# The last of four channel tiles of a causal convolution, moved from TensorE to VectorE

## The chip, the cores and the metric

The kernel runs on one core of a Trainium2 chip. The metric is the device time of one execution in microseconds, the median of several runs. The engines of the core are called PE (TensorE), DVE (VectorE), ACT (ScalarE), POOL (GpSimd) and SP (SyncE, which only issues DMAs here). Each runs its own list of instructions in order, and they meet at semaphores.

## What is computed

The program is a two-layer decoder trunk over 512 positions of 1024 channels, in float32. The first layer mixes with a state-space branch and a convolution branch side by side, the second with attention; after each mixer comes a norm, then a mixture of 64 experts (MoE) and another norm. The change lies in the convolution branch of the first layer, which works on 512 channels:

```
def conv_branch(v, cv_w, cv_b, ln_g, ln_b):
    val, gate = jnp.split(v, 2, axis=-1)
    h = val * jax.nn.sigmoid(gate)
    h = lax.conv_general_dilated(h, cv_w[:, None, :].astype(h.dtype), (1,), [(CONV_WIDTH - 1, 0)],
                                 dimension_numbers=('NWC', 'WIO', 'NWC'),
                                 feature_group_count=D_CONV) + cv_b
    return jax.nn.silu(layer_norm(h, ln_g, ln_b))

def even_mixer(x, w_in, b_in, ...):
    h = x @ w_in + b_in
    y_a = s5_branch(h[..., :D_S5], ...)
    y_b = conv_branch(h[..., D_S5:], cv_w, cv_b, cv_ln_g, cv_ln_b)
    return jnp.concatenate([y_a, y_b], axis=-1) @ w_out
```

The convolution is depthwise, causal, 31 taps wide: each output channel at position s is the sum of 31 products of one weight and the same channel at positions s-30 to s, plus a bias. The MoE after it scores 64 experts for every position and takes the best eight, so how many blocks of rows it works through depends on the data.

## The kernel before

Everything is kept channel by position: a tile is 128 channels (partitions) by 512 positions, so the 512 channels of the convolution are CT = 4 channel tiles, t = 0 to 3. The first mixer has three stages, each a function with a block of its own. A block ends in a barrier of all five engines, so the next one starts when the slowest engine is through.

**even_in_project** makes the input products on PE. For every convolution tile two products (gate, then value) are made; ACT takes the sigmoid of the gate (L1200) and DVE multiplies it with the value (L1312) into e.h2. This is a pair of buffers in which the tile is kept for PE: 64 channels stand twice in the 128 partitions of one buffer, the second copy shifted by one position, so that one matmul contracts over two taps. So DVE writes each tile with four instructions on 64 partitions. After the last product PE makes the last group of small matmuls (L1144), which ACT copies out (L1188).

**s5_and_conv** holds the state-space branch and the convolution. On PE in this order: the products into the states (L1372), conv(0), then within and across (L1391, L1401) for both halves of the states, then conv(1), conv(2), conv(3). conv(t) is 2 x 16 matmuls (L1382) of a 128 by 64 diagonal matrix of taps with the 512 positions, summed in one PSUM bank; the trace has two records for each. DVE builds the diagonals (L1434, two instructions a tile), works through the state chain twice (L1448 to L1463), and then builds the diagonals of tiles 1 to 3. ACT copies each convolution tile out of PSUM with the bias added (L1422, L1425). SP sends the results of the state-space branch to memory and back to change their layout (L1352, L1356).

**even_finish** sums the four convolution tiles on PE for the mean (L1494), and has the gated product (L1505), the variance (L1502), the norm and the activations. Then the MoE part begins.

Of the kernel before, what the change touches and what calls it, by code (L numbers as in the profile page):

```python
# [11 lines left out]
ALU, ACT, AX = mybir.AluOpType, mybir.ActivationFunctionType, mybir.AxisListType  # L12
# [5 lines left out]
P = 128  # L18
SEQ, D, NT = 512, 1024, 4
# [4 lines left out]
HP = P // 2  # L24
# [967 lines left out]


DS5, G, GS, NS = 512, 32, 16, 64
TAPS, CT = 31, 4
NJ = G * NS // P
LC = P // GS
NCH = SEQ // LC
NPAIR = (TAPS + 1) // 2
# [3 lines left out]
TWO_PI = 6.283185  # L1003

COLS = {}
for _name, _n in (("b_in", 12), ("b_glu", 4), ("cv_b", 4), ("ln_g", 4), ("ln_b", 4), ("taps", CT * 2 * NPAIR),
                  ("lam_re", NJ), ("lam_im", NJ), ("log_dt", NJ), ("skip", CT), ("power", LC + 1), ("chunk_time", NCH),
                  ("ident2", HP)):
    COLS[_name] = (sum(b - a for a, b in COLS.values()), sum(b - a for a, b in COLS.values()) + _n)
# [3 lines left out]
def even_layout(w):  # L1013

    col = lambda v: np.ascontiguousarray(v.reshape(-1, P).T)
    state = lambda v: v.reshape(NJ, P).T
    across = lambda v: np.repeat(np.asarray(v, np.float32)[None, :], P, 0)
    taps = np.concatenate([w["cv_w"][0], np.zeros((1, DS5), np.float32)]).reshape(NPAIR, 2, CT, 2, HP)
    parts = [col(w["ev_b_in"][0]), col(w["s5_b_glu"][0]), col(w["cv_b"][0]), col(w["cv_ln_g"][0]), col(w["cv_ln_b"][0]),
             taps.transpose(1, 4, 2, 3, 0).reshape(P, CT * 2 * NPAIR),  # L1020
             state(w["s5_lam_re"][0]), state(w["s5_lam_im"][0]),
             state(np.repeat(w["s5_log_dt"][0][:, None], NS, 1)), col(w["s5_d"][0]),
             across(np.arange(LC + 1)), across(LC * np.arange(NCH)), np.tile(np.eye(HP, dtype=np.float32), (2, 1))]
    b = np.stack([w["s5_b_re"][0], w["s5_b_im"][0]])
    c = np.stack([w["s5_c_re"][0], w["s5_c_im"][0]])
    b = b.reshape(2, NJ, P, GS).transpose(2, 0, 1, 3)
    c = c.transpose(0, 1, 3, 2).reshape(2, NJ, P, GS).transpose(2, 0, 1, 3)
    return np.ascontiguousarray(np.concatenate(parts, axis=1)), np.ascontiguousarray(b), np.ascontiguousarray(c)
# [24 lines left out]
def even_in_project(nc, g, w, e):  # L1053
    with Part(nc, "evin") as s:
# [3 lines left out]
        sig = s.sb("sig", [P, 2, SEQ])  # L1058
        names = ("dt", "ld", "th", "km", "k", "r", "rho", "are", "aim", "den", "rden", "fre", "fim", "t1", "t2", "t3", "t4")
        v = {n: s.sb(n, [P, NJ]) for n in names}  # L1060
# [4 lines left out]
        bank = [s.ps(f"bank{k}", [P, 512]) for k in range(8)]  # L1065
# [4 lines left out]
        sig_ready, h_ready = s.sem("sig_ready"), s.sem("h_ready")  # L1070
# [5 lines left out]
        col = e.col  # L1076
# [130 lines left out]
        def _(dve):  # L1207
# [96 lines left out]
            for t in range(CT):  # L1304
                n = 5 + 2 * t
                dve.wait_ge(done, n + 1)
                dve.wait_ge(sig_ready, t + 1)
                for k in range(2):
                    rows = slice(HP * k, HP * k + HP)
                    for a in range(2):  # L1310
                        at = TAPS - 1 - a
                        last = dve.scalar_tensor_tensor(e.h2[k][HP * a:HP * a + HP, t, at:at + SEQ], bank[2 + n % 6][rows, :],  # L1312
                                                        col["b_in"][rows, 4 + t:5 + t], sig[rows, t % 2, :], ALU.add, ALU.mult)
                last.then_inc(h_ready, 1)


def s5_and_conv(nc, g, e, yT):


    with Part(nc, "s5") as s:  # L1320
# [3 lines left out]
        prod = s.sb("prod", [P, 4, HALF, NCH])  # L1324
        decays = s.sb("decays", [P, NJ, NCH])
        ysb = e.into[:].rearrange("p j c s -> p (j c s)")[:, 0:G * NCH].rearrange("p (g k) -> p g k", k=NCH)
        diag = g.wide[:].rearrange("p k d -> p (k d)").rearrange("p (t v n c) -> p t v n c", t=CT, v=2, n=NPAIR)
        bV = [[s.ps(f"bV{h}{k}", [P, 512]) for k in range(2)] for h in range(2)]
        bY = [s.ps(f"bY{k}", [P, 512]) for k in range(4)]
        dve_steps = Chain(s.sem("dve_steps"))  # L1330
# [2 lines left out]
        diag_ready, conv_done, conv_copied = s.sem("diag_ready"), s.sem("conv_done"), s.sem("conv_copied")  # L1333
        y_done, y_copied, y_stored = s.sem("y_done"), s.sem("y_copied"), [s.sem(f"y_stored{h}") for h in range(2)]
        y_moved = s.sem("y_moved")
        col = e.col
        block = s.stack.enter_context(nc.Block())
        taps = col["taps"].rearrange("p (t v n) -> p t v n", t=CT, v=2)
        conv_bank = [bV[0][0], bV[0][1], bV[1][0], bV[1][1]]

        @block.sync
        def _(sp):
# [21 lines left out]
        @block.tensor  # L1364
        def _(pe):
            for h in range(2):
                for n in range(HALF):
                    j = HALF * h + n
                    for k in range(2):
                        for q in range(2):  # L1370
                            rows = slice(HP * q, HP * q + HP)
                            mm = pe.matmul(bV[h][k][rows, n * NCH:(n + 1) * NCH], e.into[:, j, k, rows], e.u[:, 2 * j + q, :],  # L1372
                                           start=True, stop=True)
                mm.then_inc(v_done, 1)

            def conv(t):
                pe.wait_ge(diag_ready, t + 1)
                pe.wait_ge(rotated, t // 2 + 1)
                for n in range(NPAIR):
                    for k in range(2):  # L1380
                        rows = slice(HP * k, HP * k + HP)
                        mm = pe.matmul(conv_bank[t][rows, :], diag[:, t, k, n, :], e.h2[k][:, t, 2 * n:2 * n + SEQ],  # L1382
                                       start=(n == 0), stop=(n == NPAIR - 1))
                mm.then_inc(conv_done, 1)

            def within(h):
                pe.wait_ge(toep_ready, 16 * 2 * LC)
                for n in range(HALF):
                    for q in range(2):
                        gr = 2 * (HALF * h + n) + q  # L1390
                        pe.matmul(bY[2 * h + q][:, n * NCH:(n + 1) * NCH], toep[:, gr, :], e.u[:, gr, :], start=(n == 0), stop=False)  # L1391

            def across(h):
                pe.wait_ge(padded, 1)
                pe.wait_ge(state_ready, h + 1)
                for n in range(HALF):
                    j = HALF * h + n
                    for k in range(2):
                        for q in range(2):
                            rows = slice(HP * q, HP * q + HP)  # L1400
                            mm = pe.matmul(bY[2 * h + q][:, n * NCH:(n + 1) * NCH],  # L1401
                                           e.outof[k][rows, j, 1:LC + 1, :].rearrange("p l h -> p (l h)"), state[rows, k, j, 0:NCH],
                                           start=False, stop=(n == HALF - 1 and k == 1))
                mm.then_inc(y_done, 1)

            conv(0)
            for h in range(2):
                within(h)
                across(h)
            for t in range(1, CT):  # L1410
                conv(t)

        @block.scalar
        def _(act):
            for b in range(4):
                h, q = b // 2, b % 2
                act.wait_ge(y_done, h + 1)
                act.activation(ysb[:, G // 2 * h:G // 2 * (h + 1), :].rearrange("p (j q) k -> p q j k", q=2)[:, q],
                               bY[b][:, :].rearrange("p (j k) -> p j k", k=NCH), ACT.Copy).then_inc(y_copied, 1)
                if b == 1:  # L1420
                    act.wait_ge(conv_done, 1)
                    act.activation(yT[:, CT, :], conv_bank[0][:, :], ACT.Identity, bias=col["cv_b"][:, 0:1]).then_inc(conv_copied, 1)  # L1422
            for t in range(1, CT):
                act.wait_ge(conv_done, t + 1)
                act.activation(yT[:, CT + t, :], conv_bank[t][:, :], ACT.Identity, bias=col["cv_b"][:, t:t + 1]).then_inc(conv_copied, 1)  # L1425

        @block.vector
        def _(dve):
# [3 lines left out]
            def diagonals(t):  # L1432
                for k in range(2):
                    last = dve.tensor_tensor(diag[:, t, k], col["ident2"].unsqueeze(1).to_broadcast([P, NPAIR, HP]),  # L1434
                                             taps[:, t, k, :].unsqueeze(2).to_broadcast([P, NPAIR, HP]), ALU.mult)
                last.then_inc(diag_ready, 1)
# [4 lines left out]
            for h in range(2):  # L1441
# [20 lines left out]
                link(dve.tensor_tensor(p2, p3, cos, ALU.mult))  # L1462
                dve.tensor_tensor(state[:, 1, js, 1:], p0, p2, ALU.add).then_inc(state_ready, 1)  # L1463
                dve.wait_ge(state_ready, h + 1)
            for t in range(1, CT):
                diagonals(t)


def even_finish(nc, g, w, e, yT):
# [579 lines left out]
```

## Time and profile before

| what | value |
|---|---|
| median of 3 runs | 2174.11 us |
| lowest, highest | 2172.31, 2174.54 us |
| the profiled execution | 2178.51 us |
| its span, first to last instruction | 2176.7 us |
| PE busy | 2030.0 us, 93% |
| DVE busy | 738.9 us, 34% |
| ACT busy | 402.4 us, 18% |
| mean granted clock of PE | 0.972 |

The span is what the trace covers; the profiled execution took 1.8 us more than its span. Its time is 4.4 us over the median of the runs, so lengths inside it are subtracted from its own time and the outcome is carried over to the median. A busy time is a share of the whole span and says nothing of a single stage: the rows further down are read stage by stage. Matmuls are pipelined, so the duration of one (592 ns) is longer than the step from one to the next.

### The profile page before, as it was taken

The numbers are of one execution on the slowest core, as the hardware profiler recorded it, in microseconds if no ns is written. First come the engines' busy times: TensorE is split into PE (matmuls) and PEld (weight loads), VectorE is DVE, ScalarE is ACT, GpSimd is POOL, SyncE is SP. The second block draws the span as 40 slices with busy tenths as digits, with TensorE's granted clock in tenths as the row PEclk, the third lists the DMA queues.
The fourth block names the chain that finished last, engine by engine and source line by source line (L and its number), as shares of the span: only waits on it lengthen the run. The fifth ranks groups of instructions, "written<-read, shape, count | busy, mean of one in ns | idle before, by whom it ended". The sixth has DMA issues, their size and how long they took to land. (4 is left out here: it accounts for less than half of the span.)

```text
span 2176.7 us, 26609 instructions
## 1 busy us (share of the span) xinstructions
PE 2030.0 (93%) x8690; PEld 1013.7 (47%) x8690; DVE 738.9 (34%) x1991; ACT 402.4 (18%) x881; POOL 263.1 (12%) x253
## 2 busy tenths in 40 slices
PE   8999998999999999987998888898999999999976
PEld 4553454444444444433448455554444444444432
DVE  4662252222222222225110777544222222222216
ACT  2102121111111111110001556311111111111110
POOL 0000300111111111100210000300111111111110
PEclk9999999999999999988998899999999999999998
DMA  6132245999999999969100100215799999999957
GB/s 223 10 61 97 102 160 213 397 408 413 405 407 385 413 392 382 391 244 330 20 0 29 51 2 1 86 56 231 301 393 406 410 411 406 402 412 407 398 222 326
DMA packets 107425, 566.08 MB, mean 260 GB/s; under 512 B 38624, under 2 KB 39392, under 8 KB 69088
## 3 DMA queue, kind: packets, MB, share of 16 engines
q1 hardware_dynamic: 79136, 498.06, 57.8%
q0 software_dynamic: 28224, 67.16, 7.9%
q8 instruction: 41, 0.67, 0.1%
q14 instruction: 24, 0.20, 0.0%
HBM read 539.84 MB, written 59.77 MB: 275 GB/s over the span
## 5 line engine op out<-in xcount | busy, mean ns | idle before, releaser
L438 PE MATMUL moe_bank<-moe_weights,moe_xgT 128*128 128x512 f32 x1024 | 460.0, 602 | 15.9 <-DMA moe_weights<-in_ex_weights 15.5
L438 PEld LDWEIGHTS moe_bank<-moe_weights,moe_xgT 128*128 128x128 f32 x1024 | 191.0, 192 | 234.6 <-issue 217.8
L746 DVE TENSOR_TENSOR moe_hid<-moe_sil,moe_bank 128x256 f32<-128x256 f32 x98 | 41.3, 421 | 664.1 <-ACT moe_sil L621 664.1
L471 PE MATMUL moe_bank<-moe_weights,moe_hidT 128*128 128x512 f32 x512 | 230.5, 593 | 0.0
L441 PE MATMUL moe_bank<-wide,moe_xgT 128*64 128x512 f32 x512 | 226.6, 595 | 0.0
L441 PE MATMUL moe_bank<-moe_weights,moe_xgT 128*64 128x512 f32 x512 | 226.6, 595 | 0.0
L314 POOL DMA_INDIRECT y<-moe_xy,moe_rows x98 | 98.7, 1007 | 948.1 <-DVE moe_idx L726 549.5
L621 ACT ACTIVATE moe_sil<-moe_bank 128x256 f32<-128x256 f32 x98 | 37.7, 384 | 660.8 <-PE moe_bank L438 459.4
L754 DVE TENSOR_SCALAR moe_xy<-moe_bank,moe_sgate 128x512 f32<-128x512 f32 x98 | 73.5, 750 | 219.5 <-PE moe_bank L471 142.1
L471 PEld LDWEIGHTS moe_bank<-moe_weights,moe_hidT 128*128 128x128 f32 x512 | 92.4, 191 | 93.4 <-issue 93.4
L420 PEld LDWEIGHTS moe_bank<-const_sb,moe_xy 128*128 128x128 f32 x784 | 101.0, 192 | 68.0 <-issue 49.9
L299 POOL DMA_INDIRECT moe_xy<-h,moe_idx x98 | 99.9, 1019 | 269.1 <-DVE moe_idx L726 241.3
L441 PEld LDWEIGHTS moe_bank<-moe_weights,moe_xgT 128*64 128x64 f32 x512 | 67.5, 137 | 128.8 <-issue 127.9
L347 PE MATMUL moe_bank<-wide,xT 128*128 128x512 f32 x256 | 114.1, 602 | 7.6 <-PEq L46 7.6
L633 ACT ACTIVATE moe_xy<-moe_bank,moe_sgate 128x512 f32<-128x512 f32 x98 | 67.4, 687 | 290.8 <-PE moe_bank L471 190.7
L474 PE MATMUL moe_bank<-moe_weights,moe_hidT 128*64 128x512 f32 x256 | 116.7, 598 | 1.9 <-ACT moe_hidT L625 1.9
L420 PE MATMUL moe_bank<-const_sb,moe_xy 128*128 128x128 f32 x784 | 108.0, 281 | 10.2 <-DMA moe_xy<-h,moe_idx 10.2
L474 PE MATMUL moe_bank<-wide,moe_hidT 128*64 128x512 f32 x256 | 116.7, 598 | 0.0
L347 PEld LDWEIGHTS moe_bank<-wide,xT 128*128 128x128 f32 x256 | 48.4, 193 | 65.2 <-issue 65.2
L1844 PE MATMUL att_bT<-const_sb,att_prob 128*128 128x128 f32 x320 | 55.4, 303 | 24.0 <-DVE att_prob L1976 19.3
L1911 ACT ACTIVATE att_prob<-att_prob,att_low 128x128 f32<-128x128 f32 (+3 forms) x128 | 70.4, 551 | 35.0 <-DVE att_low L1937 35.0
L739 DVE COPY moe_xgT<-moe_bank 128x512 f32<-128x512 f32 x98 | 67.8, 692 | 19.4 <-PE moe_bank L420 19.0
(348 smaller groups left out, 2422.5 us busy)
## 6 DMA issues: line engine op xcount, KB each, us to landing
moe_weights<-in_ex_weights SPq DMA_DIRECT2D x96, 2048.0 KB, 19.3
moe_weights<-in_ex_weights SPq DMA_DIRECT2D x96, 1024.0 KB, 17.2
wide<-in_ex_weights SPq DMA_DIRECT2D x34, 2048.0 KB, 22.1
wide<-in_ex_weights SPq DMA_DIRECT2D x34, 1024.0 KB, 14.6
moe_weights<-y SPq DMA_DIRECT2D x18, 1024.0 KB, 21.2
wide<-y SPq DMA_DIRECT2D x8, 1024.0 KB, 7.8
moe_xy<-y SPq DMA_DIRECT2D x6, 1024.0 KB, 27.0
oddin_win<-in_od_w_in_heads SPq DMA_DIRECT2D x1, 4288.0 KB, 20.2
```

The costliest lines, as they stand in the source:

```text
L299: pool.indirect_dma_start(out=xg[k], out_offset=None, in_=h_dram[0:SEQ, :], in_offset=IndirectOffsetOnAxis(ap=idx[k][:, 0:1], axis=0), bou ...
L314: pool.indirect_dma_start(out=y_dram[:, :], out_offset=IndirectOffsetOnAxis(ap=rows[k][:, 0:1], axis=0), in_=y[k], in_offset=None, bounds_ ...
L347: mm = pe.matmul(bout[n % 4][:, :], g.xT[:, k, i * P:(i + 1) * P], g.wide[:, k, h * 512:(h + 1) * 512], start=(k == 0), stop=(k == KC - 1))
L420: mm = pe.transpose(bX[n // 4][:, (n % 4) * P:(n % 4 + 1) * P], xg[k].rearrange("t (k c) -> t c k", c=KC)[:, n, :], c["ident"])
L438: mm = pe.matmul(bG[:, :], xgT[:, n, :], wgu[j][:, :, n, :], start=(n == 0), stop=(n == KC - 1))
L441: mm = pe.matmul(bG[HP * h:HP * h + HP, :], xgT[:, n, HP * h:HP * h + HP], wgu[2 + h][:, :, n, :], start=(n == 0), stop=(n == KC - 1))
L471: mm = pe.matmul(bY[half][:, :], hidT[:, n, :], wdn[j][:, n, cols], start=(n == 0), stop=(n == HC - 1))
L474: mm = pe.matmul(bY[half][HP * h:HP * h + HP, :], hidT[:, n, HP * h:HP * h + HP], wdn[2 + h][:, n, cols], start=(n == 0), stop=(n == HC - 1))
L633: act.activation(y[k][:, 0:512], bY[0][:, :], ACT.Copy, scale=sgate[k][:, 0:1]).then_inc(y_a, 1)
L739: dve.tensor_copy(xgT[:, 4:8, :].rearrange("p k t -> p (k t)"), bX[1][:, :]).then_inc(xT_v, 1)
L754: dve.tensor_scalar(y[k][:, 512:1024], bY[1][:, :], sgate[k][:, 0:1], None, ALU.mult).then_inc(y_v, 1)
L1911: act.activation(prob[k % 3][:, hb, 0:width], prob[k % 3][:, hb, 0:width], ACT.Exp, scale=-1.0, bias=low[k % 2][:, hb:hb + 1], accum_out=t ...
```

## The change

The last channel tile, t = 3, is no longer computed by PE. In even_in_project DVE writes it with one instruction on 128 partitions as a plain copy (128 channels, once) into the first of the two e.h2 buffers. In s5_and_conv conv(3), the two diagonals of tile 3 and ACT's copy of tile 3 are gone. DVE gets a function plain_conv, which runs after the diagonals of tiles 1 and 2: 31 taps, one instruction each, into two sums that take turns (one in yT, one in a free part of g.wide), and one addition of the two sums. From the third tap on each instruction waits for the one two places ahead of it; the final addition waits for all. The table of constants has the taps of tile 3 in a plain layout, one column fewer in all.

```diff
@@ constants @@
-TAPS, CT = 31, 4
+TAPS, CT, PLAIN = 31, 4, 1
+PAIRED = CT - PLAIN
...
-for _name, _n in (("b_in", 12), ("b_glu", 4), ("cv_b", 4), ("ln_g", 4), ("ln_b", 4), ("taps", CT * 2 * NPAIR),
+for _name, _n in (("b_in", 12), ("b_glu", 4), ("cv_b", 4), ("ln_g", 4), ("ln_b", 4), ("taps", PAIRED * 2 * NPAIR), ("plain_taps", PLAIN * TAPS),
@@ even_layout @@
-             taps.transpose(1, 4, 2, 3, 0).reshape(P, CT * 2 * NPAIR),
+             taps[:, :, :PAIRED].transpose(1, 4, 2, 3, 0).reshape(P, PAIRED * 2 * NPAIR),
+             w["cv_w"][0].reshape(TAPS, CT, P)[:, PAIRED:].transpose(2, 1, 0).reshape(P, PLAIN * TAPS),
@@ even_in_project, vector @@
                 n = 5 + 2 * t
                 dve.wait_ge(done, n + 1)
                 dve.wait_ge(sig_ready, t + 1)
+                if t >= PAIRED:
+                    dve.scalar_tensor_tensor(e.h2[0][:, t, TAPS - 1:TAPS - 1 + SEQ], bank[2 + n % 6][:, :],
+                                             col["b_in"][:, 4 + t:5 + t], sig[:, t % 2, :], ALU.add, ALU.mult).then_inc(h_ready, 1)
+                    continue
                 for k in range(2):
@@ s5_and_conv @@
-        diag = g.wide[:].rearrange("p k d -> p (k d)").rearrange("p (t v n c) -> p t v n c", t=CT, v=2, n=NPAIR)
+        wide_flat = g.wide[:].rearrange("p k d -> p (k d)")
+        diag = wide_flat[:, 0:PAIRED * 2 * NPAIR * HP].rearrange("p (t v n c) -> p t v n c", t=PAIRED, v=2, n=NPAIR)
+        odd_sums = wide_flat[:, PAIRED * 2 * NPAIR * HP:PAIRED * 2 * NPAIR * HP + PLAIN * SEQ].rearrange("p (t s) -> p t s", t=PLAIN)
...
+        taps_v = s.sem("taps_dve")
...
+        plain_taps = col["plain_taps"].rearrange("p (t n) -> p t n", t=PLAIN)
         conv_bank = [bV[0][0], bV[0][1], bV[1][0], bV[1][1]]
+
+        def plain_conv(eng, t, taps_done):
+            sums = [yT[:, CT + t, :], odd_sums[:, t - PAIRED, :]]
+            for n in range(TAPS):
+                shifted, tap = e.h2[0][:, t, n:n + SEQ], plain_taps[:, t - PAIRED, n:n + 1]
+                if n == 0:
+                    eng.tensor_scalar(sums[0], shifted, tap, col["cv_b"][:, t:t + 1], ALU.mult, ALU.add).then_inc(taps_done, 1)
+                elif n == 1:
+                    eng.tensor_scalar(sums[1], shifted, tap, None, ALU.mult).then_inc(taps_done, 1)
+                else:
+                    eng.wait_ge(taps_done, n - 1)
+                    eng.scalar_tensor_tensor(sums[n % 2], shifted, tap, sums[n % 2], ALU.mult, ALU.add).then_inc(taps_done, 1)
+            eng.wait_ge(taps_done, TAPS)
+            eng.tensor_tensor(sums[0], sums[0], sums[1], ALU.add).then_inc(taps_done, 1)
@@ s5_and_conv, tensor @@
-            for t in range(1, CT):
+            for t in range(1, PAIRED):
                 conv(t)
@@ s5_and_conv, scalar @@
-            for t in range(1, CT):
+            for t in range(1, PAIRED):
                 act.wait_ge(conv_done, t + 1)
@@ s5_and_conv, vector @@
-            for t in range(1, CT):
+            for t in range(1, PAIRED):
                 diagonals(t)
+            plain_conv(dve, CT - 1, taps_v)
```

DVE at the end of even_in_project, before. Each row is an instruction (x2: two alike in a row), output <- inputs and its size; even_h2_0 and even_h2_1 are the two buffers, bank7 and bank5 hold the value products; the branches are the borders of the blocks.

```order
L1312 SCALAR_TENSOR_TENSOR even_h2_0<-evin_bank5,even_cols,evin_sig 64x512 x2
L1312 SCALAR_TENSOR_TENSOR even_h2_1<-evin_bank5,even_cols,evin_sig 64x512 x2
L1312 SCALAR_TENSOR_TENSOR even_h2_0<-evin_bank7,even_cols,evin_sig 64x512 x2
L1312 SCALAR_TENSOR_TENSOR even_h2_1<-evin_bank7,even_cols,evin_sig 64x512 x2
L42 UNCONDITIONAL_BRANCH
L1427 UNCONDITIONAL_BRANCH
```

The same place after the change:

```order
L1318 SCALAR_TENSOR_TENSOR even_h2_0<-evin_bank5,even_cols,evin_sig 64x512 x2
L1318 SCALAR_TENSOR_TENSOR even_h2_1<-evin_bank5,even_cols,evin_sig 64x512 x2
L1311 SCALAR_TENSOR_TENSOR even_h2_0<-evin_bank7,even_cols,evin_sig 128x512
L42 UNCONDITIONAL_BRANCH
L1451 UNCONDITIONAL_BRANCH
```

Four instructions of the last tile became one; nothing else moved there.

DVE at the end of s5_and_conv, before, from the last two instructions of the state chain into even_finish (wide holds the diagonals):

```order
L1462 TENSOR_TENSOR s5_prod<-s5_prod,even_cosk 128x512
L1463 TENSOR_TENSOR s5_state<-s5_prod 128x8x64
L1434 TENSOR_TENSOR wide<-even_cols 128x1024 x6
L42 UNCONDITIONAL_BRANCH
L1508 UNCONDITIONAL_BRANCH
L1510 MEMSET evfin_eps 128x1
```

The same place after the change (xT is the tensor that the functions call yT; the pair of L1361 goes on to the 31st tap):

```order
L1487 TENSOR_TENSOR s5_state<-s5_prod 128x8x64
L1458 TENSOR_TENSOR wide<-even_cols 128x1024 x4
L1356 TENSOR_SCALAR xT<-even_h2_0,even_cols 128x512
L1358 TENSOR_SCALAR wide<-even_h2_0,even_cols 128x512
L1361 SCALAR_TENSOR_TENSOR xT<-even_h2_0,even_cols,xT 128x512
L1361 SCALAR_TENSOR_TENSOR wide<-even_h2_0,even_cols,wide 128x512
```

Two diagonals fewer, and behind them 32 instructions more: 2 TENSOR_SCALAR, 29 SCALAR_TENSOR_TENSOR and one TENSOR_TENSOR (L1363). On PE the last 32 matmuls of L1382 are gone and everything else stands as it did.

## Rows read from the trace of the kernel before

**Rows 1.** Timeline of PE, end of even_in_project to even_finish: start us, length us, group.

```profile
109.79 1.94 PE L1144 MATMUL evin_bank<-even_outof,even_bdiag 128*32 128x128 f32 x16
120.83 13.95 PE L1382 MATMUL s_bV<-even_h,wide 128*64 128x512 f32 x64 [1.46 <-DVE s_prod L1452]
149.59 41.43 PE L1382 MATMUL s_bV<-even_h,wide 128*64 128x512 f32 x192
192.55 3.67 PE L1494 MATMUL evfin_bM<-xT,const_sb 128*128 128x512 f32 x8 [1.53 <-PEq L46]
```

**Rows 2.** Timeline of DVE, the same stretch.

```profile
109.90 3.04 DVE L1312 SCALAR_TENSOR_TENSOR even_h<-evin_bank,even_cols,evin_sig 64x512 f32<-64x512 f32 x4 [14.81 <-PE evin_bank L1156]
113.87 2.36 DVE L1434 TENSOR_TENSOR wide<-even_cols 128x1024 f32<-128x1024 f32 x2 [0.93 <-PEq L46]
138.74 6.90 DVE L1434 TENSOR_TENSOR wide<-even_cols 128x1024 f32<-128x1024 f32 x6
192.58 0.06 DVE L1510 MEMSET evfin_eps<- 128x1 f32 x1 [46.94 <-PEq L46]
192.58 2.74 DVE L1512 SCALAR_TENSOR_TENSOR xT<-even_uT,even_cols,xT 128x512 f32<-128x512 f32 x4
```

**Rows 3.** Timeline of ACT, the same stretch.

```profile
111.76 0.59 ACT L1188 ACTIVATE even_kern<-evin_bank 32x512 f32<-32x512 f32 x1 [8.34 <-PE evin_bank L1144]
191.06 0.69 ACT L1425 ACTIVATE xT<-s_bV,even_cols 128x512 f32<-128x512 f32 x1 [13.05 <-PE s_bV L1382]
```

**Rows 4.** Timeline of SP's DMA queue, the last sends and the next stage's loads.

```profile
157.10 0.81 SPq L1356 DMA_DIRECT2D xT<-y_s  x2
192.51 0.39 SPq L1488 DMA_DIRECT2D evfin_wglu<-in_s_w_glu  x1
192.95 0.51 SPq L937 DMA_DIRECT2D wide<-in_ev_w_out  x1
```

**Rows 5.** Stretches: us, busy of PE, PEld, DVE, ACT, POOL, granted clock, DMA share, GB/s.

```profile
120.80:142.00 21.20, 21.16 (x160) 12.59 (x160) 20.75 (x27) 0.00 (x0) 0.00 (x0) 1.00 0.46 54
150.00:160.00 10.00, 10.00 (x50) 3.32 (x48) 0.00 (x0) 0.79 (x2) 0.00 (x0) 1.00 0.64 158
160.00:170.00 10.00, 10.00 (x50) 3.35 (x48) 0.00 (x0) 0.69 (x1) 0.00 (x0) 1.00 0.00 0
198.00:200.00 2.00, 1.91 (x4) 1.01 (x5) 0.74 (x2) 1.98 (x5) 0.00 (x0) 0.84 1.01 401
200.00:202.00 2.00, 2.00 (x3) 0.67 (x2) 0.00 (x0) 1.01 (x1) 0.00 (x0) 0.50 1.00 401
202.00:204.00 2.00, 2.00 (x5) 0.91 (x4) 0.00 (x0) 0.00 (x0) 0.00 (x0) 0.81 1.01 389
222.00:224.00 2.00, 1.05 (x2) 0.56 (x3) 0.06 (x1) 0.18 (x1) 1.09 (x2) 0.50 0.04 14
224.00:226.00 2.00, 2.00 (x4) 0.95 (x3) 0.00 (x0) 0.00 (x0) 1.94 (x4) 0.50 0.90 289
226.00:228.00 2.00, 2.00 (x5) 0.78 (x4) 0.00 (x0) 0.00 (x0) 2.00 (x2) 0.83 0.98 264
```

**Rows 6.** Groups of L1382, L1434 and L1456, 113 to 200 us: count, busy, mean ns.

```profile
L1382 PE MATMUL s_bV<-even_h,wide 128*64 128x512 f32 x256 | 55.4, 592 | 1.5 <-DVE s_prod L1452 1.5
L1434 DVE TENSOR_TENSOR wide<-even_cols 128x1024 f32<-128x1024 f32 x8 | 9.3, 1218 | 1.0 <-PEq L46 0.9
L1456 DVE TENSOR_TENSOR_SCAN s_prod<-s_decays,s_prod 128x512 f32<-128x512 f32 x2 | 2.4, 1224 | 0.1
```

**Rows 7.** Groups of DVE by form over the whole span, those nearest to the added ones.

```profile
L754 DVE TENSOR_SCALAR moe_xy<-moe_bank,moe_sgate 128x512 f32<-128x512 f32 x98 | 73.5, 750 | 219.5 <-PE moe_bank L471 142.1 <-PE moe_bank L474 77.4
L1976 DVE TENSOR_SCALAR att_prob<-att_prob,att_coef 128x512 f32<-128x512 f32 x32 | 13.4, 481 | 0.3
L1512 DVE SCALAR_TENSOR_TENSOR xT<-even_uT,even_cols,xT 128x512 f32<-128x512 f32 x4 | 2.7, 748 | 0.0
```

**Rows 8.** Chain of waits in the last MoE layer: start us, length us.

```profile
1591.75 7.02 PE moe_bank L441 x32
...
1627.26 7.02 PE moe_bank L441 x32
...
1818.04 7.13 PE moe_bank L438 x16
...
1854.10 6.28 PE moe_bank L438 x14
```

More of the change, by code:

```diff
@@ L1335, in s5_and_conv @@
         y_moved = s.sem("y_moved")
+        taps_v = s.sem("taps_dve")
         col = e.col
         block = s.stack.enter_context(nc.Block())
-        taps = col["taps"].rearrange("p (t v n) -> p t v n", t=CT, v=2)
+        taps = col["taps"].rearrange("p (t v n) -> p t v n", t=PAIRED, v=2)
+        plain_taps = col["plain_taps"].rearrange("p (t n) -> p t n", t=PLAIN)
         conv_bank = [bV[0][0], bV[0][1], bV[1][0], bV[1][1]]
+        def plain_conv(eng, t, taps_done):
[11 more added lines that the diff above has]
+            eng.tensor_tensor(sums[0], sums[0], sums[1], ALU.add).then_inc(taps_done, 1)
         @block.sync
```

## The prediction, made before the changed kernel was run

> **What bounds the kernel now.** The page gives PE 93% busy and DVE 34%, but the change lies in one stage, so what counts is which engine ends that stage and the one before it. The chain of waits that the profile prints goes back only into the last layer, so I read these stages from the timelines of the engines, in the order in which the stage is handed on.
>
> First PE's timeline [rows 1]. In s5_and_conv it starts conv(0) at 120.83 us; from there to the end of conv(3) at 149.59 + 41.43 = 191.02 it has no pause worth the name: the stretches show it busy 21.16 of 21.20 us and then 10.00 of 10.00 twice, all at a granted clock of 1.00, which is the 2.4 GHz level [rows 5]. Then ACT's timeline [rows 3]: the copy of tile 3 starts at 191.06, right behind the last matmul, and ends at 191.75. Then who comes after: even_finish starts on PE at 192.55, on DVE at 192.58 and on SP at 192.51, all at once, which is the barrier [rows 1, 2, 4]. What the others were doing tells who had kept it waiting: DVE's last work was the diagonals, over at 138.74 + 6.90 = 145.64, and its row at 192.58 says that it had then been idle for 46.94 us [rows 2]. SP issued its last sends at 157.10 [rows 4], and between 160 and 170 us the DMA engines moved nothing [rows 5], so those had landed too. The stage ends with PE's convolution tiles and a short ACT copy behind them, and DVE is free for its last 45 us. That is the room the change uses.
>
> At the end of even_in_project it is the other way round. PE is through at 109.79 + 1.94 = 111.73 [rows 1], ACT at 111.76 + 0.59 = 112.35 [rows 3], and DVE, with its four writes of tile 3, at 109.90 + 3.04 = 112.94 [rows 2]. The next block begins at 113.87, 0.93 us after DVE [rows 2]. DVE is last there, by 0.59 us.
>
> **The change part by part.**
>
> *PE's tile goes.* The three tiles in a row take 41.43 us [rows 1], so one takes 41.43 / 3 = 13.81 us. The group gives the same check: 256 records over four tiles, 64 a tile, 55.4 us busy, 55.4 / 4 = 13.85 [rows 6]. All of it is on the path, because PE has no pause ahead of it and the copy by ACT hangs on its end. ACT's copy of tile 3 also goes, but a copy of tile 2 then stands last with the same 0.69 us: nothing won there. In the clock of the old trace PE then ends at 177.21 and ACT at 177.94 (before shifting both by what the stage before it gains). Term: **-13.81 us**, if nothing else is later than 177.94.
>
> *DVE's plain convolution comes.* It starts after four of the six diagonal instructions. Six take 6.90 us with 1.22 for a single one [rows 2, 6], so the step is (6.90 - 1.22) / 5 = 1.14 and four end at 138.74 + 3 x 1.14 + 1.22 = 143.37. Its parts:
> - 2 TENSOR_SCALAR of 128x512 with a per-partition scalar from SBUF: 0.48 us each by the same form in the attention; the same operation out of PSUM costs 0.75 [rows 7]. I take 0.48, because source and target lie in SBUF: 0.96 us, at most 1.5.
> - 29 SCALAR_TENSOR_TENSOR of 128x512, two float32 tensors from SBUF and a per-partition scalar. The form is in the trace: L1512, 0.748 us each, and four in a row take 2.74 [rows 2, 7], so the step is (2.74 - 0.75) / 3 = 0.66. The wait is for the instruction two ahead, so two may overlap as in L1512: 28 x 0.66 + 0.75 = 19.2 us. Without any overlap it is 29 x 0.748 = 21.7.
> - the last addition, 0.75 at most by the same row.
>
> Together 0.96 + 19.2 + 0.75 = 20.9 us, ending at 164.3; without overlap 23.4 us, ending at 166.8. Against 177.94 that leaves 13.6 or 11.1 us of cover. So the added work costs **0**, and the cover is PE's conv(1) and conv(2). It would be gone from (177.94 - 143.37) / 32 = 1.08 us an instruction on. Queued behind plain_conv on DVE is only the barrier. PE waits for nothing in it, since conv(1) and conv(2) need only the diagonals that are built ahead of it. Reading the same e.h2 buffer that PE streams is not quite what DVE did before, but in 120.80 to 142.00 DVE was busy 20.75 us beside PE's 21.16 and PE kept its rate [rows 5]; conv(0) took 13.95 there against 13.81 for the later ones that had no DVE beside them, and the 0.14 is about what the tail of a pipelined row adds [rows 1]. From below, two tiles at 0.14 each would cost 0.28 us; I leave that to the range.
>
> *The write of tile 3.* Four instructions on 64 partitions took 3.04 us. One on 128 partitions has as many elements per partition, so it costs what one of the four does, 0.75 by the nearest row of the form [rows 7], and ends at 110.65. ACT at 112.35 becomes last, so the barrier comes 112.94 - 112.35 = 0.59 us earlier: **-0.59 us**; between nothing and that if barrier work hides it.
>
> *The rest.* Two diagonals fewer: they ended at 145.64 in the open, no one waits. The constants are one column shorter: nothing. even_finish reads the same tensors; its two loads are issued at its start [rows 4] and shift with it, as does all that follows. The work of the later stages is the same and depends on this one only through the barrier, so no later stage takes the gain back.
>
> *Sum.* 13.81 + 0.59 = 14.40 us. The profiled execution then takes 2178.51 - 14.40 = 2164.1, with a span of 2162.3. The median of the runs is 4.4 us below that execution; carried over: 2174.11 - 14.40 = **2159.7 us**.
>
> **A rule that speaks against it.** The trace has this instruction form at 748 ns, the same as others of 512 elements [rows 7]. The Trainium skill, Vector Engine (DVE) Microarchitecture Reference, section "Points that are easy to get wrong", says that the scalar_tensor_tensor layout "with two non-bf16 SBUF sources halves throughput". All 29 have two float32 sources in SBUF. The trace disagrees with this rule, because L1512 has exactly that.
>
> **The rivals.**
>
> *DVE becomes last.* L1512 reads its sources from aligned starts, while plain_conv reads e.h2 at offsets 0 to 30; the trace has no two-source operation like this. Should each take double the stream, the nearest row is the scan of the same size, 1.224 us [rows 6]: 29 x 1.224 + 1.5 + 0.75 = 37.7 us, DVE ends at 181.1, 3.2 us after ACT. The gain is 14.4 - 3.2 = 11.2: 2162.9 us. Against it stands L1512. By that page's rule it is this case. To be slower than before by this road DVE would have to end past 191.75 + 0.59, which is (192.34 - 143.37) / 32 = 1.53 us an instruction, and no row of this size costs that.
>
> *The clock after the pauses.* Between blocks PE pauses, and after that the granted clock stands at 0.50, the 1.2 GHz level, for some time: around 200 us and around 224 us [rows 5]. What is lost there, as the windows' missing share of 2 us each: 2 x (0.16 + 0.50 + 0.19) = 1.7 us, and with 1.05 us busy in the first window 0.5 + 1.0 + 0.3 = 1.8 us. PE's run ahead of these pauses is 14 us shorter and their place moves. If both low stretches fell away the time would be 2156.2, if both doubled 2163.2. For it: the first stretch sets in only some 3 us behind the end of L1494 at 196.22 us [rows 1], so a shift can move it off or onto busy work. Against: PE still has over 27 us without a pause ahead of the barrier.
>
> *More rounds in the MoE: the slower case.* DVE sums the taps in another order than PE, which changes the last digits of the tile and so the scores by which experts are picked. If one position changes an expert whose row count stands just at a block's border, the layer needs another block, and if its rounds are full, another round. The trace has 98 steps in its row of L754 [rows 7], 49 a layer, which is 16 rounds of 3 and one. A round costs 1627.26 - 1591.75 = 35.5 us where PE binds and 1854.10 - 1818.04 = 36.1 where the weights do [rows 8]: 2159.7 + 35.8 = 2195.5 us. It decides from a single row over the border on; nothing in the trace shows how near one is, but rounding has to hit a near tie and the border both.
>
> *The gain doesn't come.* If something besides PE held the stage until 191 us, only the 0.59 us would show: 2173.5. DVE's 46.94 us idle and the DMA engines' empty stretch speak against it [rows 2, 5].
>
> **How the numbers follow.** The forecast with its clock variants: 0.88. DVE last: 0.06. Another round: 0.02. No gain: 0.02. What I have not thought of: 0.02, half of it slower. The predicted time is the forecast's, 2159.7. The range runs from 2156.0 (both low stretches gone) to 2164.5 (DVE last, 2162.9, and 1.6 us more out of the 2.2 us by which the runs shown differ). About 0.2%, 4.3 us, is what a measurement of this kernel can tell from no change. Faster by more: 0.88 + 0.06 and half of the unknown, cut by 0.01 for a forecast that ends near the border, 0.94. Within: 0.03. Slower: 0.03.
>
> **What would show each step right or wrong.** On PE one group of 128 records of L1382's kind, 27.6 us, right behind the state products; if it is longer, DVE's reading disturbs it. On DVE the group of 29 with a mean near 0.75 us and a total near 19 to 22 us, ending some 13 us ahead of ACT's last copy, and an idle time of about 14 us ahead of even_finish in place of 46.94. If that idle time is near nothing, DVE is last. The first block's border at 113.3 in place of 113.87, behind ACT. The steps of L754 still 98; 101 would be another round. The prediction is wrong if a DVE tap costs over 1.08 us, if PE's tiles lose their step of 13.81, or if the time between even_finish's start and the end is not the old one.

## The result

The changed kernel took 2160.88 us, the median of four runs (2158.83 to 2161.61), against 2174.32 us before: a ratio of 0.9936 with a 95% interval of 0.9921 to 0.9952, 13.4 us faster where 14.4 were forecast. In two more groups of runs it took 2162.81 and 2162.60 us. Over all 13 runs its median is 2161.6, against 2173.7 for 52 runs of the kernel before: 12.1 us. The direction, the mechanism and the range held; the sum was 1 to 2.3 us too large, and the experiments look for where that went.

TensorE around the changed place, after (start us, length us, group; L1396 are the state products, L1406 the convolution, L1519 the first matmuls of even_finish). They answer to [rows 1]:

```profile
112.46 3.95 PE L1396 MATMUL s_bV<-even_u,even_into 128*64 128x64 f32 x128 [1.53 <-PEq L46]
119.43 13.96 PE L1406 MATMUL s_bV<-even_h,wide 128*64 128x512 f32 x64 [3.01 <-DVE s_prod L1476]
148.18 27.69 PE L1406 MATMUL s_bV<-even_h,wide 128*64 128x512 f32 x128
177.41 3.67 PE L1519 MATMUL evfin_bM<-xT,const_sb 128*128 128x512 f32 x8 [1.54 <-PEq L46]
```

VectorE and ScalarE, after, which answer to [rows 2, 3]:

```profile
109.10 0.75 DVE L1311 SCALAR_TENSOR_TENSOR even_h<-evin_bank,even_cols,evin_sig 128x512 f32<-128x512 f32 x1 [14.81 <-PE evin_bank L1158]
112.46 2.36 DVE L1458 TENSOR_TENSOR wide<-even_cols 128x1024 f32<-128x1024 f32 x2 [2.61 <-PEq L46]
141.88 0.54 DVE L1356 TENSOR_SCALAR xT<-even_h,even_cols 128x512 f32<-128x512 f32 x1
162.06 0.69 DVE L1363 TENSOR_TENSOR xT<-xT,wide 128x512 f32<-128x512 f32 x1
177.44 0.06 DVE L1535 MEMSET evfin_eps<- 128x1 f32 x1 [14.68 <-PEq L46]
...
110.96 0.59 ACT L1190 ACTIVATE even_kern<-evin_bank 32x512 f32<-32x512 f32 x1 [8.34 <-PE evin_bank L1146]
175.92 0.69 ACT L1449 ACTIVATE xT<-s_bV,even_cols 128x512 f32<-128x512 f32 x1 [13.05 <-PE s_bV L1406]
```

The last tile's 64 records are gone, and ScalarE's copy of tile 2 (175.92) hands the block on. VectorE began the taps at 141.88, ended at 162.75 and was then idle for 14.68 us, where it had been idle for 46.94. The first border too is as foreseen: VectorE is through at 109.85, ScalarE at 111.55, and the next block begins 0.9 us behind ScalarE, not VectorE. All 29 two-source tap instructions took the same, 743 to 745 ns:

```profile
L1361 DVE SCALAR_TENSOR_TENSOR xT<-even_h,even_cols,xT x15: 743/743/745, 142.7 to 161.3; 128x512 f32<-128x512 f32 x15
L1361 DVE SCALAR_TENSOR_TENSOR wide<-even_h,even_cols,wide x14: 743/743/745, 143.4 to 160.6; 128x512 f32<-128x512 f32 x14
```

The two spans differ by 19.7 us, more than the medians. The profiled execution before was a long one of its kernel (2178.51), the one after the shortest. A difference of two whole profiles is no result here; lengths within one block can be compared.

### The profile page after: what moved, and what is told of

It is laid out like the page before. It is cut to its first block and busy times, and to the rows that moved or that the text cites. A ratio compares the mean times of both kernels' runs of the same rounds, so it can differ in the third digit from the quotient of the medians.

```text
span 2157.0 us, 26506 instructions
## 1 busy us (share of the span) xinstructions
PE 2008.3 (93%) x8626; PEld 1004.3 (47%) x8626; DVE 757.6 (35%) x2018; ACT 401.4 (19%) x880; POOL 263.5 (12%) x253
## 5 line engine op out<-in xcount | busy, mean ns | idle before, releaser
L754 DVE TENSOR_SCALAR moe_xy<-moe_bank,moe_sgate 128x512 f32<-128x512 f32 x98 | 73.6, 751 | 219.5 <-PE moe_bank L471 142.1
```

The costliest lines, as they stand in the source:

```text
L754: dve.tensor_scalar(y[k][:, 512:1024], bY[1][:, :], sgate[k][:, 0:1], None, ALU.mult).then_inc(y_v, 1)
```

## The experiments

There were twelve more runs: nine further kernels, the changed kernel twice and the kernel before once more. In what follows a ratio is to the kernel before in the same group. "The block" is s5_and_conv, from the start of its first matmul to the start of the first one of even_finish; a low stretch is one in which TensorE's granted clock is at 0.50, the 1.2 GHz level.

**The changed kernel again.**

> The changed kernel once more, beside the others of this group. My sum (one tile on PE, 13.81 us, and 0.59 us at the border ahead of it) expects the kernel before minus 14.4 us, a ratio of 0.9934. In the profile the block with the convolution again begins some 0.7 us behind ACT's last copy, and that with the norm some 15 us earlier than before. The rival that part of the gain was the clock's expects a profile in which the 1.2 GHz stretch behind the mean's matmuls, gone in the first profile of this kernel, may be back, worth 1.7 us.

Median 2162.81 us (five runs, 2159.01 to 2165.67), ratio 0.9942 (0.9928 to 0.9957). The low stretch in even_finish is back (5.35 us for the first eight matmuls of L1530, 3.70 in the first profile), and there is one that I had not looked for, on conv(0). The execution profiled is the longest of the five. TensorE, then stretches (us, busy of PE, PEld, DVE, ACT, POOL, then the granted clock, DMA share and GB/s):

```profile
113.24 3.95 PE L1396 MATMUL s_bV<-even_u,even_into 128*64 128x64 f32 x128 [1.53 <-PEq L46]
120.20 15.65 PE L1406 MATMUL s_bV<-even_h,wide 128*64 128x512 f32 x64 [3.02 <-DVE s_prod L1476]
179.88 3.67 PE L1519 MATMUL evfin_bM<-xT,const_sb 128*128 128x512 f32 x8 [1.54 <-PEq L46]
...
120.00:122.00 2.00, 1.80 (x6) 0.70 (x8) 1.97 (x4) 0.00 (x0) 0.00 (x0) 0.72 0.34 72
122.00:124.00 2.00, 2.00 (x8) 0.76 (x6) 1.97 (x3) 0.00 (x0) 0.00 (x0) 0.50 0.26 42
124.00:126.00 2.00, 2.00 (x12) 0.84 (x10) 1.93 (x4) 0.00 (x0) 0.00 (x0) 0.93 0.66 111
```

Behind the 3.02 us pause in which TensorE waits for VectorE, conv(0) ran 1.7 us longer, at 1.2 GHz for part of it, and everything behind it on the path moved by that: the block takes 179.88 - 113.24 = 66.64 us, against 177.41 - 112.46 = 64.95 in the first profile.

**The taps left out.**

```diff
-            plain_conv(dve, CT - 1, taps_v)
+            dve.tensor_copy(yT[:, CT + CT - 1, :], e.h2[0][:, CT - 1, TAPS - 1:TAPS - 1 + SEQ]).then_inc(taps_v, 1)
```

> The changed kernel without the 31 taps and the final addition on VectorE: one copy of 128x512 stands in their place, so channel tile 3 is not convolved. Theory: the taps are wholly covered by TensorE's two tiles, so the time equals that of the changed kernel within 1 us, and VectorE's idle time ahead of the norm's block grows from 14.7 us to about 35. Rival: the taps disturb TensorE, since both read the same buffer; then TensorE's group of 128 records (27.69 us with the taps) gets shorter here by what they cost, and the whole by as much.

```profile
112.36 3.95 PE L1396 MATMUL s_bV<-even_u,even_into 128*64 128x64 f32 x128 [1.53 <-PEq L46]
148.07 27.69 PE L1406 MATMUL s_bV<-even_h,wide 128*64 128x512 f32 x128
177.30 3.67 PE L1519 MATMUL evfin_bM<-xT,const_sb 128*128 128x512 f32 x8 [1.53 <-PEq L46]
...
177.33 0.06 DVE L1535 MEMSET evfin_eps<- 128x1 f32 x1 [35.13 <-PEq L46]
```

From the start of the block to the next it is 177.30 - 112.36 = 64.94 us, against 64.95 with the taps, and TensorE's group is 27.69 in both. The taps cost nothing and disturb nothing: the rival falls. The whole took 2164.12 us (ratio 0.9951, 0.9937 to 0.9965), 1.3 us more than the changed kernel in this group, where I had expected at most 1; the two intervals overlap, so no difference is shown. With a tile left unconvolved the data behind it are others, so I take the block alone.

**TensorE's tile left out of the kernel before** (conv, diagonals and ScalarE's copies each stop one tile earlier; VectorE copies tile 3 unconvolved in their place).

> The kernel before with conv(3), its two diagonals and its copy by ScalarE left out: channel tile 3 is not convolved (a plain copy of the buffer stands for it), and VectorE still writes it with four instructions. Theory: this is the first term alone, 13.81 us less than before, 2160.5; the border ahead stays 0.93 us behind VectorE's write, so it is 0.6 us slower than the changed kernel without its taps. Rival: if the tile's removal is worth less than its 13.81 us because later stages give it back, the time lies above 2162.

```profile
113.78 5.50 PE L1372 MATMUL s_bV<-even_u,even_into 128*64 128x64 f32 x128 [2.14 <-PEq L46]
178.82 3.67 PE L1495 MATMUL evfin_bM<-xT,const_sb 128*128 128x512 f32 x8 [1.53 <-PEq L46]
```

The block takes 65.04 us; before it took 192.55 - 113.87 = 78.68 [rows 1, 2]. The first term measures 13.6 to 13.7 us. The total (2167.95, ratio 0.9962, 0.9948 to 0.9976; 2160.5 expected) met the rival's condition, that the time lies above 2162. The profiles say where the excess is: from the start of even_finish to the end of the span this kernel takes 2166.9 - 178.82 = 1988.1 us and the one without taps 1989.6, while the kernel before took 1984.2 and 1977.5 in its two profiles and the changed one 1979.6, 1983.9 and 1981.0 in its three. So it is the two kernels with tile 3 unconvolved that are longer there, and the changed kernel, which convolves all four tiles, shows nothing given back there. The data are the likely reason, which is not shown: both have the same 98 steps of the MoE (L754) as all the others.

**The taps computed twice** (plain_conv called again with its waits counted on).

> The changed kernel with VectorE computing tile 3 twice, one after the other (32 instructions more, the same result). Theory: the cover of TensorE ends at 176.6 us; VectorE with 20.9 us more ends at 183.7 and becomes last, so the norm's block begins 7 us later and the whole takes 7.0 us more than the changed kernel, about 2168. Rival, if something else held the block's end: no change, or a full 20.9 us more if there were no cover at all.

```profile
182.91 0.69 DVE L1363 TENSOR_TENSOR xT<-xT,wide 128x512 f32<-128x512 f32 x1
184.45 0.06 DVE L1537 MEMSET evfin_eps<- 128x1 f32 x1 [0.85 <-PEq L46]
...
112.29 3.95 PE L1396 MATMUL s_bV<-even_u,even_into 128*64 128x64 f32 x128 [1.53 <-PEq L46]
119.35 16.82 PE L1406 MATMUL s_bV<-even_h,wide 128*64 128x512 f32 x64 [3.11 <-DVE s_prod L1476]
184.42 6.44 PE L1521 MATMUL evfin_bM<-xT,const_sb 128*128 128x512 f32 x8 [5.77 <-PEq L46]
```

VectorE is last now: idle only 0.85 us ahead of the border. The block takes 184.42 - 112.29 = 72.13 us, 7.2 more than with one round of taps (7.0 expected), out of 20.9 added. The total is 2166.14 us (ratio 0.9962, 0.9948 to 0.9975), 3.3 more than the changed kernel in this group, where 7.0 were expected. Part of the missing 3.7 us: conv(0) took 16.82 here and cost nothing, because TensorE was not last, while a slow conv(0) does cost the changed kernel: against its profile in this group the block is 72.13 - 66.64 = 5.5 us longer. No run settles the rest.

**The four writes of tile 3 put back.** The single write is again four on 64 partitions, two of them into the unused part of the second buffer.

> The changed kernel with tile 3 written by four instructions on 64 partitions again (two of them into a part of the buffer that nobody reads), as before the change; the taps stay on VectorE. It undoes the second term alone. My sum: the border comes 0.6 us later, so 0.6 us slower than the changed kernel. Rival, the clock theory from the profiles of the last group: with the border 0.6 us later TensorE's pause there is 2.1 us again, the 1.2 GHz stretch falls on the state products (5.5 us, off the path) and conv(0) always takes 13.95 us, where the changed kernel showed 13.96, 15.65 and, with the taps doubled, 16.82. By that the time equals the changed kernel's or is up to 1.5 us less.

```profile
113.17 3.95 PE L1400 MATMUL s_bV<-even_u,even_into 128*64 128x64 f32 x128 [2.15 <-PEq L46]
120.14 16.92 PE L1410 MATMUL s_bV<-even_h,wide 128*64 128x512 f32 x64 [3.02 <-DVE s_prod L1480]
```

Median 2160.68 (six runs, 2158.38 to 2163.61), ratio 0.9938 (0.9926 to 0.9950): not slower. TensorE's pause at the border grew by 0.6 us (1.53 to 2.15) as both theories have it, so the second term is real; it is too small to be seen in the total. But my rival said that conv(0) would then always be fast, and here it took 16.92. So the length of the border's pause does not alone decide where the low stretch falls. That part of the theory is wrong.

**The pause ahead of conv(0) filled** with six extra matmuls.

```diff
+            for n in range(6):
+                pe.matmul(bY[3][:, :], e.h2[0][:, 0, 0:P], e.h2[0][:, 0, 0:SEQ], start=True, stop=True)
             conv(0)
```

> The changed kernel with six extra matmuls of 128x512 (2.6 us, results unused) in TensorE's pause of 3.0 us ahead of conv(0). Clock theory: the pause is what lets the clock fall on conv(0); with it filled conv(0) takes 13.95 us at a granted clock of 1.00, at unchanged start, and the median is 1 to 2 us below the changed kernel's. Rival, that the clock falls for another reason: conv(0) is as often slow, the time the same or worse.

```profile
116.29 5.42 PE L1431 MATMUL s_bY<-even_h 128*128 128x512 f32 x12
121.64 13.95 PE L1406 MATMUL s_bV<-even_h,wide 128*64 128x512 f32 x64
```

Each matmul of this form runs as two records, so six take 5.4 us and not 2.6: conv(0) began 2.3 us late, 9.23 us after the block's start in place of 6.97. It took 13.95, yet with the late start nothing is won: 2161.91 us (2158.65 to 2162.47), ratio 0.9940 (0.9927 to 0.9953). The size was my error. In this profile the clock held; since it also held in some profiles without the extra matmuls, this one alone doesn't prove that they did it.

**conv(0) in another bank,** without the wait, ScalarE copying it first.

```diff
-        conv_bank = [bV[0][0], bV[0][1], bV[1][0], bV[1][1]]
+        conv_bank = [bY[3], bV[0][1], bV[1][0], bV[1][1]]
...
-                pe.wait_ge(rotated, t // 2 + 1)
+                if t:
+                    pe.wait_ge(rotated, t // 2 + 1)
```

> The changed kernel with conv(0) summed in a PSUM bank that the state products don't use, so that it need not wait until VectorE has read them; ScalarE copies it out ahead of its other work, and the second half's matmuls wait for that copy. The pause of 3.0 us ahead of conv(0) goes. Theory: TensorE's tiles still end the block, so the norm's block begins 3.0 us earlier, and the clock cannot fall on conv(0): 3 to 4.5 us less than the changed kernel, 2157 to 2159. Rival: TensorE now waits for the state chain of VectorE (ready at 137.3 us, wanted at 141.4) or VectorE's taps (end 162.8, against 173.6) become last: then less.

Neither: 2173.50 us, the median of 11 runs, ten from 2170.4 to 2175.4 and one at 2159.5 (ratio 0.9992, 0.9978 to 1.0005). The whole gain of the change was gone. TensorE, then the clock:

```profile
116.52 13.94 PE L1407 MATMUL s_bY<-even_h,wide 128*64 128x512 f32 x64
132.49 6.84 PE L1416 MATMUL s_bY<-even_u,s_toep 128*128 128x64 f32 x32 [2.04 <-DMA s_toep<-even_kern]
139.26 7.09 PE L1426 MATMUL s_bY<-s_state,even_outof 64*128 64x64 f32 x64
146.28 7.09 PE L1416 MATMUL s_bY<-even_u,s_toep 128*128 128x64 f32 x32
153.30 7.09 PE L1426 MATMUL s_bY<-s_state,even_outof 64*128 64x64 f32 x64
160.32 29.25 PE L1407 MATMUL s_bV<-even_h,wide 128*64 128x512 f32 x128
...
134.00:138.00 4.00, 4.00 (x20) 4.00 (x21) 3.86 (x7) 0.00 (x0) 0.00 (x0) 0.50 0.00 0
150.00:160.00 10.00, 10.00 (x80) 9.88 (x79) 10.00 (x16) 0.00 (x0) 0.00 (x0) 0.50 0.37 88
160.00:164.00 4.00, 4.00 (x14) 1.35 (x14) 3.12 (x5) 1.09 (x2) 0.00 (x0) 0.56 0.20 35
164.00:168.00 4.00, 4.00 (x22) 1.30 (x20) 0.00 (x0) 0.00 (x0) 0.00 (x0) 1.00 0.55 101
```

conv(0) starts 3.2 us earlier, counted from the block's start, but now TensorE is at the Toeplitz blocks (s_toep, the matrices of the first small matmuls) before their DMA has landed, pauses 2.04 us, and the clock falls to 0.50. It stays there through all four groups of small matmuls, which were 3.79 us each before, and comes back only within the 512-column matmuls of conv(1).

**That pause bridged** with three extra matmuls behind conv(0).

> The kernel with conv(0) in another bank, and three extra matmuls of 128x512 (2.6 us, results unused) behind conv(0), in the 2.0 us in which TensorE waited there for the last of the Toeplitz blocks. Theory: that pause is what dropped the clock to 0.50, and the small matmuls that follow never brought it back (four groups at 6.8 to 7.1 us in place of 3.79) until conv(1); bridged, all four groups take 3.79 us and the whole takes 2160 to 2161, 13 us less than without the bridge and with no second level. Rival, that the small matmuls lose the clock by themselves when they start that early: the groups stay near 7 us and the time near 2173.

```profile
130.09 2.84 PE L1437 MATMUL s_bY<-even_h 128*128 128x512 f32 x6
132.77 3.68 PE L1416 MATMUL s_bY<-even_u,s_toep 128*128 128x64 f32 x32
136.38 3.79 PE L1426 MATMUL s_bY<-s_state,even_outof 64*128 64x64 f32 x64
147.53 27.69 PE L1407 MATMUL s_bV<-even_h,wide 128*64 128x512 f32 x128
```

2158.72 us (2156.16 to 2159.90), ratio 0.9928 (0.9915 to 0.9942): 2.84 us of unused work save 14.8 us by the medians, which come from two groups (13.9 by the ratios). The small matmuls start within 0.6 us of where they did without the bridge, counted from the block's start, and all take 3.7 to 3.8 us, so the rival falls: the pause ahead of them is the cause. None of the five runs is near 2173. Against the changed kernel (0.9949, 0.9934 to 0.9964 in the same group) the intervals overlap.

**Six tap pairs of tile 2 moved to VectorE as well,** on a plain copy in the unused part of the second buffer.

> The changed kernel with the last six tap pairs of tile 2 (11 taps) moved to VectorE too, on a plain copy of tile 2 in an unused part of the buffer; VectorE adds TensorE's sum to its own at the end. TensorE's run gets 6 x 0.86 = 5.2 us shorter (to about 170.7), VectorE's 7.7 us longer (to about 170.5) and one addition of 0.7 us stands in place of ScalarE's copy. Theory, cover at a known rate: the norm's block begins 5 us earlier, 2156 to 2157. Rival: the two together disturb each other near balance, and half of that is lost.

```profile
148.05 22.54 PE L1430 MATMUL s_bV<-even_h,wide 128*64 128x512 f32 x104
172.22 3.67 PE L1544 MATMUL evfin_bM<-xT,const_sb 128*128 128x512 f32 x8 [1.63 <-PEq L46]
...
169.47 0.69 DVE L1383 TENSOR_TENSOR wide<-wide 128x512 f32<-128x512 f32 x1
170.71 0.69 DVE L1386 TENSOR_TENSOR xT<-s_bV,wide 128x512 f32<-128x512 f32 x1 [0.54 <-PE s_bV L1430]
```

The block takes 59.98 us, 5.0 less than the changed kernel's in its first profile. TensorE ends at 170.59 and VectorE's own sums at 170.16, half a microsecond apart; the rival, that they disturb each other, falls. 2154.85 us (2151.84 to 2156.22), ratio 0.9914 (0.9901 to 0.9927).

**The same with three extra matmuls ahead of conv(0).**

> The kernel with six tap pairs of tile 2 moved to VectorE, and three extra matmuls (2.6 us, results unused) in the 3.1 us pause ahead of conv(0). Theory: conv(0) always takes 13.95 us, so the slow executions go and the median is 1 us or less below that of the split alone: 2153 to 2155. Rival: the pause left over (0.5 us) and the one at the border are enough, and nothing changes.

2152.58 us (four runs, 2149.14 to 2152.75), ratio 0.9898 (0.9883 to 0.9913), the fastest kernel of the study, 21.6 us below before in its group. Its interval and that of the split alone overlap, so what the three matmuls add is not shown by these totals. Nor do the profiles show it: conv(0) took 13.96 us in both, behind a pause of 0.34 us here and of 3.11 us in the split alone.

**Before, a second profile, and the changed kernel a third time.**

> The kernel before once more, for a second profile of it. Clock theory as it stands after the last group: where the 1.2 GHz stretch falls behind a pause changes from one execution to the next. In the first profile of this kernel it fell on the state products (5.50 us in place of 3.95), where nothing waits, and conv(0) took 13.95. If that is the rule for this kernel, this profile has the same two numbers; if it changes here as well, the state products take 3.95 us, the pause ahead of conv(0) is about 3 us and conv(0) may take up to 17.

> The changed kernel a third time, for its profile and for its median. Clock theory: the state products take 3.95 us as in its two earlier profiles, conv(0) starts at about 119.5 to 120.3 us behind a pause of 3.0 us and takes between 13.95 and 17 us; the median of all its runs stays 12 to 13 us below before, 1.5 us short of the sum.

```profile
113.53 5.50 PE L1372 MATMUL s_bV<-even_u,even_into 128*64 128x64 f32 x128 [2.14 <-PEq L46]
120.50 13.95 PE L1382 MATMUL s_bV<-even_h,wide 128*64 128x512 f32 x64 [1.47 <-DVE s_prod L1452]
...
112.90 3.95 PE L1396 MATMUL s_bV<-even_u,even_into 128*64 128x64 f32 x128 [1.53 <-PEq L46]
119.86 15.65 PE L1406 MATMUL s_bV<-even_h,wide 128*64 128x512 f32 x64 [3.01 <-DVE s_prod L1476]
```

The first two lines are the kernel before, the others the changed one. Before was 2172.59 us (ratio to its own other runs 0.9995, 0.9985 to 1.0005) with the pattern of its first profile; the changed kernel 2162.60 (0.9949, 0.9934 to 0.9964), with conv(0) slow again.

Over all fourteen profiles: in the seven with a pause of 3.0 to 3.1 us ahead of conv(0) it took 15.65 to 16.92 us four times and 13.95 or 13.96 three times; in the seven with a pause of 1.6 us or less, or none, it always took 13.94 to 13.96. That fits the pause as the occasion of the low stretch. It is a count and no test, since three of the latter seven had their low stretch on the state products just before.

## Why the prediction was right, and where it was off

- **What bounds the block.** Right. TensorE ended it before and after, with ScalarE's short copy behind it, and with one or no round of taps the block's length is the same to 0.01 us (64.95 and 64.94, both with conv(0) at full clock).
- **TensorE's tile, 13.81 us.** Right: 78.68 - 64.95 = 13.73 us in the two first profiles, 13.64 with the tile merely left out. The 13.81 was a third of a row that also holds the tail of its last matmul; two rows subtracted, 41.43 - 27.69, give 13.74.
- **The cover of VectorE's taps.** Right to 0.3 us: 20.9 us forecast, 162.75 - 141.88 = 20.87 measured, with 13.9 us to the end of ScalarE's copy (13.6 forecast). The instruction took 743 ns as the row of L1512 had it; offsets of 0 to 30 elements change nothing. The Trainium skill, Vector Engine (DVE) Microarchitecture Reference, "Points that are easy to get wrong", has the throughput of such an instruction halved with two non-bf16 SBUF sources. The trace disagrees: 743 ns for 512 elements and 0.66 us from start to start, where the prediction's rival had 1.224 us and VectorE last. The point at which the cover ends was shown with the doubled taps, 7.2 us for 7.0.
- **The border, 0.59 us.** Right: 109.10 + 0.75 ends ahead of ScalarE, and TensorE's pause there fell from 2.14 to 1.53 us, by 0.61.
- **"No later stage takes the gain back."** For the later stages this holds as far as the profiles can tell: they took 1984.2 and 1977.5 us before and 1979.6, 1983.9 and 1981.0 after. The sum was off ahead of the tile. I had looked for the clock only behind the block. In the kernel before the low stretch lies on the state products (5.50 us, in both its profiles and in the one with its tile left out, with a pause of 1.5 us behind them and conv(0) at 13.95). The changed kernel runs them in 3.95 us. Nothing is won by that, since VectorE lets conv(0) start 6.96 or 6.97 us after the block's start in either kernel; TensorE only waits 3.0 us in place of 1.5, and the low stretch then may fall on conv(0), which is on the path. Its three profiles show 13.96, 15.65 and 15.65, a mean of 1.1 us lost. That is about half of the 2.3 us between 14.4 and the 12.1 of all runs. The prediction had put this at nothing without looking at it. The rest is within what medians of this kernel leave open (0.2% is 4.3 us), and no run settles it. That the first group came within 1 us of the sum is in part luck: the two later ones gave 11.1 and 11.6 us.
- **The rivals.** DVE last, another round (still 98 steps) and no gain: none came. The clock rival came in another place. In the place where the prediction had it, the low stretch in even_finish was gone in one profile of the changed kernel (3.70 us for the first matmuls of L1530) and there in the two others (5.35 and 5.40), as in both profiles before (5.40).

What stays open is why the kernel before had its low stretch on the state products in every profile. The border's pause alone is not it, since with the same pause (2.15 us) the four-writes kernel had it on conv(0).

## What to carry to other kernels

Price a tile moved to an idle engine by the rows of the same instruction form and compare its end with that of the engine that covers it. Where both can take single taps, split the work until they end together: that brought 5 us more in the block. Before shortening or removing a wait ahead of matmuls, ask what TensorE will wait for next and which matmuls come behind that pause. Here a wait of 3 us for VectorE ahead of the 512-column matmuls of conv(0) went with up to 3 us more for them, and a wait of 2 us ahead of four groups of small ones cost 14 to 15.

## What the runs showed of the hardware

- A pause of 2.04 us on TensorE was followed by four groups of 64-column matmuls, 27.8 us together, at a granted clock of 0.50, the 1.2 GHz level, almost from their start, although TensorE was busy without a break. The clock was at 1.00 again from 164 us on, within the 512-column matmuls that began at 160.32. The same small matmuls right behind 512-column ones, without the pause, took 14.8 us. Ten of eleven runs of that kernel have the longer time.
- 64-column matmuls don't always stay low. In the kernel before the state products (L1372, 128 records of 64 columns) began at 0.51 behind the border's pause and the clock rose while they ran:

```profile
114.00:116.00 2.00, 2.00 (x42) 2.00 (x43) 2.00 (x2) 0.00 (x0) 2.00 (x1) 0.51 0.03 8
116.00:118.00 2.00, 2.00 (x51) 2.00 (x50) 1.92 (x3) 0.00 (x0) 1.99 (x2) 0.64 0.00 0
118.00:120.00 2.00, 1.37 (x47) 1.23 (x43) 1.93 (x5) 0.00 (x0) 0.00 (x0) 1.00 0.15 16
```

  At 1.00 a record of these takes 3.95 / 128 = 0.03 us and one of the four groups 3.79 / 32 = 0.12 us. What in the four groups keeps the clock low is not shown.
- Whether a low stretch falls on conv(0) behind the same pause of 3.0 us changes from execution to execution: the changed kernel's 64 records took 13.96 us once and 15.65 twice. In variants of it they took up to 16.92.
- VectorE's two-source float32 instruction takes 0.66 us from start to start and 0.743 us by itself, with TensorE reading the same buffer beside it and its group of 128 records at 27.69 us with and without the taps.
